# A mixture-of-experts layer pair on one core: the queue of expert weights asks for the down weights first and waits for another signal

## The reference

```python
idx = lax.top_k(sel, TOP_K)[1]                  # 8 of 64 experts for each token
...
padded = (counts + MOE_BLOCK - 1) // MOE_BLOCK * MOE_BLOCK
...
def expert_block(args):                         # one block: 128 rows of one expert
    tok, e = args
    xb = h_pad[tok]
    return (jax.nn.silu(xb @ w_eg[e]) * (xb @ w_eu[e])) @ w_ed[e]
y = lax.map(expert_block, (row_tok.reshape(n_blocks, MOE_BLOCK), block_e)).reshape(n_rows, D)
routed = jnp.zeros((T + 1, D), h.dtype).at[row_tok].add(y * row_w[:, None])[:T]
```

## Time and profile before

| | |
|---|---|
| median of 3 runs | 3568.11 us (3552.45 to 3585.15) |
| the profiled execution | 3585.25 us, its span 3583.5 us |
| PE busy | 3276.0 us (91%), granted clock 0.968 |
| DVE, ACT, POOL busy | 1742.1, 1329.5, 579.1 us |
| DMA | 720.76 MB, mean 201 GB/s |
| expert stage, first layer | about 1122 to 1966 us of the span |
| expert stage, second layer | about 2804 to 3500 us |

### The profile page before, as it was taken

How to read it: one execution, slowest core, us unless ns; L and a number is a source line. 1 busy time by engine, 2 the same in 40 slices (tenths; PEclk the granted TensorE clock), 3 DMA queues, 4 the chain that set the end, 5 groups by cost and what they waited for, 6 DMA issues and landing times.

```text
span 3583.5 us, 46643 instructions
## 1 busy us (share of the span) xinstructions
PE 3276.0 (91%) x14784; PEld 2348.9 (66%) x14784; DVE 1742.1 (49%) x2411; ACT 1329.5 (37%) x1889; POOL 579.1 (16%) x751
## 2 busy tenths in 40 slices
PE   7989999999986999999998699999998799999995
PEld 3468877899643666666665347887764466666672
DVE  1353242222255666666665525343334466666764
ACT  2343142112112555555553224332211355555551
POOL 0000210000033222222222000020003222222220
PEclk9999999999998999999999899999998899999998
DMA  6310211334213999999996810102221699999985
GB/s 227 100 59 7 74 42 59 124 132 145 98 55 146 345 365 355 357 360 368 366 353 250 341 49 1 50 19 71 88 97 56 240 360 349 343 351 348 343 330 224
DMA packets 219921, 720.76 MB, mean 201 GB/s; under 512 B 55330, under 2 KB 103876, under 8 KB 163076
## 3 DMA queue, kind: packets, MB, share of 16 engines
q1 hardware_dynamic: 174628, 626.96, 47.7%
q0 software_dynamic: 45184, 92.28, 6.7%
HBM read 701.35 MB, written 84.13 MB: 219 GB/s over the span
## 4 chain that ended last, share of the span: by engine, by line
PE 71%; DMA 12%; DVE 7%; issue 4%; ACT 3%; SPq 1%; another core or an unknown queue 1%; DVEq 0%; POOLq 0%; ACTq 0%; POOL 0%
PE ps L736 11%; PE ps L738 10%; PE ps L737 10%; PE ps L805 8%; PE ps L729 7%; PE ps L758 6%; PE ps L913 4%; PE ps L932 4%; DMA region_v<-in_w_exp_up 4%; PE ps L1006 4%; DMA ring<-in_w_exp_up 3%; DMA region_k<-in_w_exp_up 3%; DMA region_h<-y_rows 2%; DVE ring_split L1422 1%; PE ps L833 1%
## 5 line engine op out<-in xcount | busy, mean ns | idle before, releaser
L758 PEld LDWEIGHTS ps<-con,region_c 128*128 128x128 f32 x1958 | 263.8, 168 | 163.3 <-issue 89.2
L758 PE MATMUL ps<-con,region_c 128*128 128x128 f32 x1958 | 291.5, 277 | 54.4 <-DMA region_c<-h_rows,idx_in 29.4
L1831 POOL DMA_INDIRECT y_rows<-region_q,idx_out x141 | 144.6, 1025 | 959.6 <-DVE region_q L1466 933.6
L738 PE MATMUL ps<-region_x_split,ring_split 128*128 128x384 f32 (+2 forms) x800 | 284.7, 356 | 0.0
L736 PE MATMUL ps<-region_h_split,region_q_split 128*128 128x512 f32 x568 | 230.7, 406 | 37.7 <-DVE ring_split L1422 37.5
L736 PE MATMUL ps<-ring_split,region_q_split 128*128 128x512 f32 x560 | 225.7, 403 | 27.8 <-DVE ring_split L1422 27.3
L1082 ACT ACTIVATE region_q<-ps 128x512 f32<-128x512 f32 (+2 forms) x157 | 99.7, 636 | 340.5 <-PE ps L805 277.6
L738 PE MATMUL ps<-region_h_split,ring_split 128*128 128x512 f32 x568 | 225.0, 396 | 0.0
L738 PE MATMUL ps<-ring_split 128*128 128x512 f32 x560 | 220.7, 394 | 0.0
L1257 ACT ACTIVATE region_c<-ps 128x768 f32<-128x768 f32 (+1 forms) x48 | 33.8, 705 | 412.1 <-PE ps L738 412.1
L1422 DVE TENSOR_TENSOR ring_split<-ps,region_q_split 128x1024 fp32r<-128x1024 f32 x141 | 171.5, 1216 | 20.7 <-ACT region_q_split L1082 20.7
(11 more groups left out here) (306 smaller groups left out, 7038.4 us busy)
## 6 DMA issues: line engine op xcount, KB each, us to landing
ring<-in_w_mod SPq DMA_DIRECT2D x24, 2048.0 KB, 8.1
region_k<-in_w_exp_gate SPq DMA_DIRECT2D x48, 1024.0 KB
region_k<-in_w_exp_up SPq DMA_DIRECT2D x48, 1024.0 KB
region_k<-in_w_exp_down SPq DMA_DIRECT2D x48, 1024.0 KB
region_v<-in_w_exp_gate SPq DMA_DIRECT2D x47, 1024.0 KB
region_v<-in_w_exp_up SPq DMA_DIRECT2D x47, 1024.0 KB
region_v<-in_w_exp_down SPq DMA_DIRECT2D x47, 1024.0 KB
ring<-in_w_exp_gate SPq DMA_DIRECT2D x46, 1024.0 KB
```

The lines of the kernel that those rows point to most:

```text
L738: last = mm(o, wl, xh, start=False, stop=k == len(stationary) - 1)
L758: last = nc.tensor.transpose(ps[0:t.shape[1], at:at + t.shape[0]], t, ident[0:t.shape[0], 0:t.shape[0]])
L1831: pool.indirect_dma_start(Y8, bass.IndirectOffsetOnAxis(ap=idx_out[:, s:s + 1], axis=0), yb[:, s, :], None, bounds_check=TOK * TOPK - 1, o ...
```

## The change

The loop of SP's queue is turned. Before it only G2 is issued; D2 is the first load in the loop. In a round, D of the block ahead comes first and waits for `y_a` (ACT has copied its half of the result of the block that held the buffer), then comes G of the block after it, which waits for `gu_done` as before. Each of the two has its own condition and reads the expert's number for itself.

```diff
-                for n in range(2, DEPTH_W):
-                    load_gate_up(expert(n), n)
-                    load_down(expert(n), n)
+                load_gate_up(expert(2), 2)
                 with sp.Fori(0, max_turns(l) // UNROLL) as m:
                     with sp.If(UNROLL * m < n_blocks):
                         for r in range(UNROLL):
-                            n = UNROLL * m + r
-                            with sp.If(n + DEPTH_W < n_blocks):
-                                e = expert(n + DEPTH_W)
-                                sp.wait_ge(sl["gu_done"], n + 1)
+                            n = UNROLL * m + r + 1
+                            with sp.If(n + 1 < n_blocks):
+                                e = expert(n + 1)
+                                sp.wait_ge(sl["y_a"], n)
+                                load_down(e, (r + 2) % DEPTH_W)
+                            with sp.If(n + 2 < n_blocks):
+                                e = expert(n + 2)
+                                sp.wait_ge(sl["gu_done"], n)
                                 load_gate_up(e, r % DEPTH_W)
-                                sp.wait_ge(sl["dn_done"], n + 1)
-                                load_down(e, r % DEPTH_W)
```

## The result

The changed kernel takes 3608.29 us (median of 4 runs, 3596.24 to 3610.32) against 3566.84 us for the kernel before (4 runs). The ratio is 1.0106, 95% interval 1.0055 to 1.0158. Timed a second time beside the kernel before (e9), it is 1.0098, interval 1.0074 to 1.0122. The forecast was 3583 us with a range of 3556 to 3608: the sign was right, the size too small by more than half, and the time lies at the upper end of the range. The run that was profiled is the fastest of the four.

A forecast was written before the change was run, and what follows sets the result against it. In the expert stages PE and a three-block loop through the weight loads were taken as near a tie; 26 up-weight flights x 0.60 us, taken as 15 us, on 3568.11 gave 3583 us, range 3556 to 3608.

The forecast's parts named there:

- That nothing is reordered: In SP's queue, turning the loop lets no load pass another, and the bytes stay the same.
- The loop of three blocks: Expert stages: down product's end, loads, up landing, matmuls, next down product on that buffer; 32.2 us against PE's 30.1 us.
- the interval of 13.88 us: Time between two down loads in SP's queue before the change, against 10.04 us at PE's own pace.
- the count of flights on the chain: Up-weight flights on the chain that ended last in both expert stages: 26, each 0.60 us later, 15.6 us in all.
- G's net delay: Gate and up request in SP's queue: 0.70 us later by the signal, 0.10 us given back by the loop's end, 0.60 net.
- the upper bound of the sum: Every expert block hanging on the three-block loop: 135 x 0.60 / 3 = 27 us, or 32 us with 0.70.
- the feedback: Rival: in expert blocks, late up weights delay ACT's result copy and so the next loads; 3610 us, chance 0.13.
- the signs named ahead: Expected in the changed profile: down loads 0.7 to 0.8 us after the product, up landing 14 to 15.2 us behind, blocks near 10.78 us.
- The rival of the backlog: Rival: in expert stages the slowest DMA engine always has work, hiding the delay; 3568 us (3565 to 3571), chance 0.25.
- The return of 0.69: Up weights asked for 3.84 us later gained back 2.66 us, 0.69 of it; not taken to apply here.
- The scatter: Rival: the scatter, issued ahead of gate and up, stops spreading landings; up to 3490 us, chance 0.06 of over 1%.
- That G alone is what counts: Expert stages: the sum charged only the gate and up request's 0.60 us delay; the down load's own 0.70 us was covered.

The follow-up runs named there:

- e9: The changed kernel itself, timed again beside the kernel before: ratio 1.0098.
- e2: Kernel before with the loop turned as in the changed kernel, but down loads still waiting for the end of the down product: ratio 1.0007.
- e1: Kernel before, loop unturned, with down loads waiting for ACT's copy of the result instead of the down product's end: ratio 1.0080.
- e5: Kernel before with down loads waiting for a still later signal, DVE's copy of the next block's hidden rows: ratio 1.0271.
- e7: Turned loop with gate and up requested ahead of down, both waiting for the end of the down product: ratio 0.9851 to the kernel before.
- e3: Kernel before with one unused value load ahead of the gate and up request, so only that request is later: ratio 1.0038.
- e10: Kernel before with three unused value loads ahead of the gate and up request, down request at its old time: ratio 1.0100.
- e6: Turned loop with the old signal, both value loads ahead of the wait, so gate and up follow down at once: ratio 1.0051 to the kernel before.
- e8: e4 with down loads waiting for ACT's copy of the result, the changed kernel's signal: ratio 0.9854 to the kernel before.
- e4: e2 with the two requests exchanged: gate and up first, as early as their own signal allows, then down: ratio 0.9868 to the kernel before.

## Why the prediction was right, and where it was short

*That nothing is reordered* held: the order is G2 D2 G3 D3 on both sides, and e2 shows that the turned loop by itself makes no difference. The description of the change speaks of an order, and only the signal changes the time.

*The loop of three blocks* held as to who waits for what. Up landed 0.70 us later behind the down product (0.64 in e9), and 139 x 0.70 / 3 = 32 us; the stage got 31 us longer (35 in e9). The same working gives 25 us for e1 (26 measured), -6 for e2 (-7), 85 for e5 (90) and -69 for e7 (-58, where PE's own pace begins to count). But it gives 4 us for e3 (8), 7 for e10 (21) and 6 for e6 (19), so the mean landing isn't all. The loop's own sum also left a term out. It gave 32.2 us from the down product that ended at 1504.00, but the one three blocks on ended near 1537.96, 33.96 us later. In that round PE ran at half its clock for a while, right behind its wait of 1.86 us (length, PE busy, clock, DMA share, GB/s):

```profile
1527.30:1530.70 3.40, 3.40 (x10) 0.50 1.00 406
```

That costs up to 1.7 us, the missing part. So the interval of 13.88 us is PE's 10.04, some 2.1 us of the loop and 1.7 us of clock.

*The term that was mis-sized* is the count of flights on the chain, 26 x 0.60 = 15.6 us. G's net delay was 0.76 us, not 0.60: on the copy's signal D is issued 0.73 us later (e1), one register operation behind the wait adds 0.14, and the loop's end gives 0.11 back. That would make 20 us. In the two profiles PE's idle time grew by 26 and 22 us, little more than that. The rest of the measured 35 to 41 us can be the clock, for which the sum has no term: the time at 1.2 GHz grew by 7 us and by 20 us, worth up to 3 and 10 us. How much of it belongs to the change is open, since two profiles of one kernel differ by that much and the timed runs of e9 show the same mean clock as those beside them (0.966, with 10 us of uncertainty). Taken together the slope is 46 us per us and not 26, and the upper bound of the sum, 0.76 x 45 = 34 us with the true delay, comes near the measured value. Whether that is because blocks which the chain gives to PE were moved too (PE and the DMA path were near a tie), or because the clock adds to a shorter wait, was not tried apart.

*The range* took the result in at its very edge, and its upper end was drawn for the feedback, which did not occur. Of the signs named ahead, SP's wait on ACT's copy, D to G without the 1.93 us and ACT's longer waits for up came as described; D came 0.90 us behind the product and not 0.7 to 0.8, up landed 14.04 us behind D, just inside 14 to 15.2, and a block took 10.92 and not 10.78 us.

*The rival of the backlog* is refuted by e1, e5 and e7: later requests land later by most of the delay (0.54 of 0.73 us in e1, 1.83 of 1.97 in e5), and the order alone moved the time by 53 us, where the bytes are the same. The return of 0.69 that I had read from two intervals didn't hold for a delay of every request, as argued. In e3 something like it did (0.56 of 0.65 us); there only G was late. *The feedback* wasn't there with ACT's copy: it ended 0.73 us behind the down product at the median in both kernels, 0.81 at the 95th percentile. e5 shows it with another signal. *The scatter* (faster) was not separated from the rest: in e6 and e7 G is ahead of the scatter and the results go opposite ways, so the place of the scatter is not what decides.

*That G alone is what counts*, silent in the sum, was not right. D and G together cost 40 to 49 us per us (e1, e9, e5), G alone 22 and 19 (e3, e10), the clock's part included. It made no difference to this forecast, since both move.

## What to carry to other kernels

When two paths are near a tie, take the chain that ended last as the lower end of what a delay costs, and the loop (here three buffers, so a third of the delay for every block) as the upper; here the total came near the loop (and in e5 slightly above it). Then compare the time that PE spends at its lower clock in the stage, by the windows of both profiles: waits can be the same and the time still be longer (e6). When a queue has a request that is urgent and one that isn't, look at which stands in front before looking at signals: exchanging the two here won 1.5% (about 2.5% against the changed kernel), more than any timing of the old order that was tried. The later signal cost 29 us where gate and up stood behind the wait (e1), and nothing that can be measured where they didn't (e8 beside e4).

## What was unexpected of the hardware

An earlier request need not land earlier: G 0.7 us sooner behind D (e6) landed no sooner, and G 5.65 us sooner (e4) landed 1.8 us sooner. A load waits for the last of its 16 landing signals, and these don't come together: for the down load issued at 1504.00 they came from 1508.43 to 1510.90, and the median from the first to the last is 2.4 us over the 74 down loads of the kernel before that have all of them in the trace.

PE's clock fell behind its waits. Before all three falls in the expert stages of the kernel before, PE had sat idle for 1.86 us just ahead, but there were eight waits of about that length, so not each of them was followed by one. In e7 and e4, where PE is idle for 12 and 19 us in all in these stages, the clock never fell.
